# Two banks, a narrower gather and a later selection in the expert loop of a two-layer encoder trunk

## The chip, the cores and the metric

The kernel runs on one core of one Trainium2 chip. The metric is the device time of one execution in microseconds, the median of several; lower is better.

## What is computed

256 tokens of width 1024 go through two layers. Layer 0 is a latent attention and a dense SwiGLU, layer 1 a stick-breaking attention and a SwiGLU with 8 experts of which each token takes two. Everything is float32. The change touches the experts alone:

```
def swiglu(h, w_gate_up, w_down):
    g, u = jnp.split(h @ w_gate_up, 2, axis=-1)
    return (jax.nn.silu(g) * u) @ w_down
...
    for e in range(N_EXPERTS):
        y = y + gates[:, e:e + 1] * swiglu(xt, w_gate_up[e], w_down[e])
```

`w_gate_up[e]` is 1024 x 5632 and `w_down[e]` 2816 x 1024, so one expert has 34.6 MB of weights.

## The kernel before

The engines are programmed by hand, each with its own instruction list in a fixed order; semaphores join them. The expert layer is a list of items. An item is one expert and the tokens routed to it: a "big" item has 128 slots, a "small" one 64. Big and small items alternate, four pairs in this run (items 0 to 7); the last two pairs are in a loop with a run-time bound (`Fori`) and in the code behind it. A "pair" below is a big item and the small item after it.

**Units.** The weights of an item come as 33 units of 1 MB (22 of gate and up, 11 of down). SyncE's queue (SP) issues their transfers, in order, into a ring `raw` of 11 slots. It may fill a slot again when its content is used: in a big item when VectorE has made `wlo` of it (`lo_made`), in a small item when TensorE has finished with it (`small_used`). `after_big` and `big_loads` hold the first rule, `after_small` and `small_loads` the second. So the first 11 units of a small item (0 to 10) go into the slots that the last 11 units of the big item leave, and unit 11 waits until TensorE has finished unit 0 of the small item.

**Big item.** ScalarE rounds a unit to `whi` (L561), VectorE takes the rest as `wlo` (L962), both in a ring of 3 units; TensorE makes three products for each block of 512 columns (L1482 to L1484), 12 matmuls a unit. ScalarE may begin unit x+3 when TensorE has finished unit x (`used`). The 2816 hidden columns are made in groups j = 0 to 5 of 512 columns (the last of 256), with a gate half and an up half each; a half fills one bank of PSUM (512 columns), groups 0 and 1 are made in units 0 to 7, groups 2 and 3 in units 8 to 15, groups 4 and 5 in units 16 to 21. ScalarE takes silu of the gate half (L773, `silu_done`), VectorE multiplies by the up half (L1225, `gated`), TensorE transposes the product, and units 22 to 32 are the down product.

**Small item.** TensorE multiplies the raw float32 weights directly (L1487), 8 matmul instructions a unit in the trace, with no split before.

**Between items.** In down unit d = 5 of every item TensorE gathers the tokens of the next item: `gather` multiplies the token rows `xm` (stationary, 128 x 128) by a selection matrix `sel` (moving, 128 columns), 16 matmuls, of which a small item reads columns 0 to 63 only. ScalarE copies the result to `xs` for a small item or to `xhi` for a big one. `selection` then transposes `sel` into bank 6 (`TR_BANK`); it waits until all 8 copies are done, since they read banks 6 and 7, and stands behind down unit d = 8. After the last down unit `begin` computes units 0 and 1 of the next item, and then the item's result is spread back to the tokens ("scatter") in banks 4 to 7.

Of the kernel before, what the change touches and what calls it, by code (L numbers as in the profile page):

```python
# [14 lines left out]
P = 128  # L15
SEQ, D = 256, 1024
TC = SEQ // P
# [36 lines left out]
SMALL = 64  # L54
# [6 lines left out]
SUB = 6  # L61
# [5 lines left out]

def sub_bank(j):

    return (0, 2, 4, 0, 2, 7)[j]  # L70


SMALL_GROUPS = 4
# [62 lines left out]
def build(nc, t, out):  # L136
    with ExitStack() as ctx:
# [11 lines left out]
        xhi = sb("xhi", [P, KD, SEQ], F32R)  # L149
# [784 lines left out]
        def _(dve):  # L934
# [284 lines left out]
            def big(i, g, following):  # L1219

                def gate(j):
                    dve.wait_ge(silu_done[2], i * SUB + j + 1)
                    w = sub_width(j)
                    up = ps[:, sub_bank(j) + 1, :] if j < SUB - 1 else ps[:, sub_bank(j), w:2 * w]
                    V.tensor_tensor(gm[:, j % 2, 0:w], up, gm[:, j % 2, 0:w], ALU.mult).then_inc(gated[2], 1)  # L1225

                def low(j):
                    dve.wait_ge(h_hi[2], i * SUB + j + 1)
                    w = sub_width(j)
                    chunks = slice(4 * j, 4 * j + w // P)  # L1230
                    V.tensor_tensor(elo[:, chunks, :].rearrange("p a s -> p (a s)"), ps[:, TR_BANK, 0:w],
                                    ehi[:, chunks, :].bitcast(F32).rearrange("p a s -> p (a s)"), ALU.subtract).then_inc(h_lo[2], 1)

                for x in range(2, FU):
                    if x in (7, 15, 21):
                        gate({7: 0, 15: 2, 21: 4}[x])
                    if x in HIDDEN_AT:
                        low(HIDDEN_AT.index(x))
                    if x == 14:
                        item_gates(g)  # L1240
                        choose(g + 1, following)
                    if x == FU - 1:
                        for m in range(2):
                            dve.wait_ge(y_hi, i * 2 + m + 1)
                            V.tensor_tensor(xlo[:, 4 * m:4 * m + 4, P:SEQ], ps[:, 4 + m, :].rearrange("p (a s) -> p a s", a=4),
                                            xhi[:, 4 * m:4 * m + 4, P:SEQ].bitcast(F32), ALU.subtract).then_inc(y_lo, 1)
                    if x + 3 < FU or following == "big":
                        split_low_unit(H_MOE + RING + 2 * x, i)
                    if x in (7, 15, 21):
                        gate({7: 1, 15: 3, 21: 5}[x])  # L1250
                    if x == 29 and following == "big":
                        gathered_low(i + 1)
                if following == "big":
                    for x in range(3, 5):
                        split_low_unit(H_MOE + 2 * x, i + 1)
                add_in(g)
# [222 lines left out]
        def _(pe):  # L1479
# [248 lines left out]
                    if f == LAST_TR:  # L1728
                        transposes(n - 1)

            def gather(g):

                pe.wait_ge(sel_ready, g * 2 + 2)
                for k in range(KD):
                    o = ps[:, 6 + k // 4, (k % 4) * P:(k % 4 + 1) * P]
                    for c in range(TC):
                        last = mm(o, xm[:, c, k * P:(k + 1) * P], sel[:, c, :], c == 0 and k % 4 == 0, c == TC - 1)
                    if k % 4 == 3:
                        last.then_inc(gathered, 1)

            def big_unit(x, i, g):

                hh = H_MOE + 2 * x
                pe.wait_ge(lo_made, i * FH + hh + 2)
                whi_x, wlo_x = unit_split(whi, x), unit_split(wlo, x)
                if x < 16:
                    k = x % 8
                    if x < 8:
                        pe.wait_ge(xe_lo, i * KD + k + 1)
                    if x == 8:  # L1750
                        pe.wait_ge(h_ready[4], g * 4 + 4)
                    for n in range(2):
                        j = 2 * (x // 8) + n
                        if k == 0 and j == 3:
                            pe.wait_ge(gated[2], i * SUB + 1)
                        for a in range(2):
                            w = slice(a * 1024 + n * 512, a * 1024 + (n + 1) * 512)
                            last = mm3(ps[:, sub_bank(j) + a, :], xhi[:, k, 0:P], xlo[:, k, 0:P],
                                       whi_x[:, w], wlo_x[:, w], k == 0, k == KD - 1)
                        if k == KD - 1 and n == 0:  # L1760
                            last.then_inc(even_done, 1)
                else:
                    if x == 16:
                        pe.wait_ge(gated[2], i * SUB + 2)
                    for place, k, a in pieces(x, 4):
                        w = slice(place, place + 512)
                        last = mm3(ps[:, sub_bank(4) + a, :], xhi[:, k, 0:P], xlo[:, k, 0:P],
                                   whi_x[:, w], wlo_x[:, w], k == 0, k == KD - 1)
                    if x == GU - 1:
                        last.then_inc(even_done, 1)  # L1770
                    for place, k, a in pieces(x, 5):
                        w = slice(place, place + 256)
                        last = mm3(ps[:, sub_bank(5), a * 256:(a + 1) * 256], xhi[:, k, 0:P], xlo[:, k, 0:P],
                                   whi_x[:, w], wlo_x[:, w], k == 0 and a == 0, k == KD - 1)
                last.then_inc(used, 2)
# [43 lines left out]
            def big(i, g, following, next_i):  # L1819

                def transposes(j):
                    pe.wait_ge(gated[2], i * SUB + j + 1)
                    if j >= 1:
                        pe.wait_ge(h_lo[2], i * SUB + j)
                    w = sub_width(j)
                    for b, block in enumerate(interleaved(gm[:, j % 2, 0:w], j)):
                        last = pe.transpose(ps[:, TR_BANK, b * P:(b + 1) * P], block, ident[:, :])  # L1827
                    last.then_inc(gu_tr[2], 1)

                for x in range(2, GU):  # L1830
                    big_unit(x, i, g)
                    if x + 1 in HIDDEN_AT:
                        transposes(HIDDEN_AT.index(x + 1))
                for d in range(FU - GU):
                    hh = H_MOE + 2 * (GU + d)
                    pe.wait_ge(lo_made, i * FH + hh + 2)
                    if d % 2 == 0:
                        pe.wait_ge(h_lo[2], i * SUB + d // 2 + 1)
                    for m in range(2):
                        for n in range(2):  # L1840
                            f = 2 * d + n
                            w = slice(m * 512, (m + 1) * 512)
                            last = mm3(ps[:, 4 + m, :], ehi[:, f, :], elo[:, f, :],
                                       w_hi(hh + n)[:, w], w_lo(hh + n)[:, w], f == 0, f == FC - 1)
                    last.then_inc(used, 2)
                    if GU + d + 1 in HIDDEN_AT:
                        transposes(HIDDEN_AT.index(GU + d + 1))
                    if d == 5:
                        pe.wait_ge(h_lo[2], i * SUB + SUB)
                        gather(g + 1)  # L1850
                    if d == 8:
                        selection(following, next_i)
                begin(following, next_i, g + 1)
                pe.wait_ge(y_lo, i * 2 + 2)
                pe.wait_ge(selN_ready, g + 2)
                pe.wait_ge(selT_ready, g + 1)
                for c in range(TC):
                    for n in range(2):
                        o = ps[:, 4 + 2 * c + n, :].rearrange("p (a s) -> p a s", a=4)
                        w = selT[:, c * P:(c + 1) * P]  # L1860
                        mm(o, w, xhi[:, 4 * n:4 * n + 4, P:SEQ], True, False)
                        mm(o, w, xlo[:, 4 * n:4 * n + 4, P:SEQ], False, True).then_inc(scattered, 1)

            def small(p, g, following, next_i):
# [16 lines left out]
                for d in range(FU - GU):  # L1881
# [12 lines left out]
                        transposes(d + 1)  # L1894
                    if d == 5 and following is not None:
                        pe.wait_ge(hT_ready, p * SMALL_GROUPS + SMALL_GROUPS)
                        gather(g + 1)
                    if d == 8 and following is not None:
                        selection(following, next_i)
                if following is not None:  # L1900
# [100 lines left out]

            keep_clock(4, 4)
            pe.wait_ge(xm_ready, 2)
            gather(0)
            keep_clock(9, 4)
            begin("big", 0, 0)
            selection("big", 0)
# [32 lines left out]
```

## Time and profile before

| | us |
|---|---|
| median of 3 runs | 1138.62 (1137.79 to 1139.3) |
| the profiled execution's own time | 1135.15 |
| its span | 1133.4 |
| TensorE busy | 1083.6 |
| VectorE busy | 627.1 |
| ScalarE busy | 522.9 |
| bytes moved | 343.47 MB |

Times of single instructions are in microseconds from the start of the span. The expert items run from about 432 to 1123 us. A TensorE instruction's own length in the trace overlaps the next, so the time that one costs is read from the distance of two starts. "Idle before" is the time for which an engine stood still ahead of an instruction, with the work that ended it. The DMA share is the mean over 16 DMA engines and can be a little over 1.

### The profile page before, as it was taken

The numbers are of one execution on the slowest core, as the hardware profiler recorded it, in microseconds if no ns is written. First come the engines' busy times: TensorE is split into PE (matmuls) and PEld (weight loads), VectorE is DVE, ScalarE is ACT, GpSimd is POOL, SyncE is SP. The second block draws the span as 40 slices with busy tenths as digits, with TensorE's granted clock in tenths as the row PEclk, the third lists the DMA queues.
The fourth block names the chain that finished last, engine by engine and source line by source line (L and its number), as shares of the span: only waits on it lengthen the run. The fifth ranks groups of instructions, "written<-read, shape, count | busy, mean of one in ns | idle before, by whom it ended". The sixth has DMA issues, their size and how long they took to land.

```text
span 1133.4 us, 15880 instructions
## 1 busy us (share of the span) xinstructions
PE 1083.6 (96%) x5832; PEld 808.5 (71%) x5832; DVE 627.1 (55%) x712; ACT 522.9 (46%) x577; POOL 23.0 (2%) x94
## 2 busy tenths in 40 slices
PE   9998999999999999999998999998999999999994
PEld 9887888888898787787355787355787355787451
DVE  6866455555654458895116895106896106897102
ACT  6555444344445644774015774015775005776001
POOL 1100000000000000000000000000000000000000
PEclk9999999999999999999999999999999999999998
DMA  9933556555454424997999999999999999999994
GB/s 347 358 114 112 186 186 188 183 186 198 162 173 148 137 75 153 371 359 269 375 419 408 402 418 409 352 416 410 403 418 409 364 414 410 404 415 409 357 413 192
DMA packets 110935, 343.47 MB, mean 303 GB/s; under 512 B 11613, under 2 KB 38282, under 8 KB 100618
## 3 DMA queue, kind: packets, MB, share of 16 engines
q1 hardware_dynamic: 110714, 341.93, 79.9%
q8 instruction: 47, 0.77, 0.3%
q10 hardware_dynamic: 144, 0.52, 0.1%
q14 instruction: 30, 0.25, 0.1%
HBM read 341.37 MB, written 1.05 MB: 302 GB/s over the span
## 4 chain that ended last, share of the span: by engine, by line
PE 77%; DMA 7%; DVE 7%; ACT 3%; issue 2%; SPq 2%; POOL 0%; POOLq 0%; ACTq 0%; DVEq 0%
PE ps L1487 20%; PE ps L1482 18%; PE ps L1484 18%; PE ps L1483 18%; DMA raw<-moe_w_gate_up_dram 5%; DMA raw<-moe_w_down_dram 2%; SPq L368 2%; ACT whi L561 2%; DVE wlo L962 1%; PE ps L1827 1%; DVE wlo L949 1%; DVE wlo L951 1%; ACT xs L561 1%; DMA raw<-mla_w_down_dram 1%; DVE h L1144 1%
## 5 line engine op out<-in xcount | busy, mean ns | idle before, releaser
L561 ACT ACTIVATE whi<-raw 128x2048 fp32r<-128x2048 f32 (+2 forms) x203 | 341.7, 1688 | 245.8 <-PE ps L1484 226.8
L962 DVE TENSOR_TENSOR wlo<-raw,whi 128x2048 fp32r<-128x2048 f32 x151 | 345.7, 2294 | 119.5 <-ACT whi L561 118.3
L1482 PE MATMUL ps<-whi,xhi 128*128 128x512 f32 (+3 forms) x688 | 264.3, 384 | 16.3 <-DVE wlo L962 9.2
L1484 PE MATMUL ps<-wlo,xhi 128*128 128x512 f32 (+3 forms) x688 | 260.2, 378 | 0.0
L1483 PE MATMUL ps<-whi,xlo 128*128 128x512 f32 (+3 forms) x688 | 259.7, 377 | 0.0
L1482 PEld LDWEIGHTS ps<-whi,xhi 128*128 128x128 f32 x688 | 129.9, 189 | 45.2 <-DVE wlo L962 8.5
L1487 PE MATMUL ps<-raw,xs 128*64 128x512 f32 (+2 forms) x1024 | 155.0, 461 | 0.0
L1484 PEld LDWEIGHTS ps<-wlo,xhi 128*128 128x128 f32 x688 | 129.6, 188 | 23.9
L1483 PEld LDWEIGHTS ps<-whi,xlo 128*128 128x128 f32 x688 | 129.8, 189 | 22.5
L1487 PEld LDWEIGHTS ps<-raw,xs 128*64 128x64 f32 x1024 | 68.2, 137 | 81.7 <-issue 71.5
L1482 PE MATMUL ps<-whi,hhi 128*128 128x512 f32 x264 | 105.9, 401 | 0.0
L1483 PE MATMUL ps<-whi,hlo 128*128 128x512 f32 x264 | 104.3, 395 | 0.0
L1484 PE MATMUL ps<-wlo,hhi 128*128 128x512 f32 x264 | 104.3, 395 | 0.0
L949 DVE TENSOR_TENSOR wlo<-raw,whi 128x1024 fp32r<-128x1024 f32 (+1 forms) x52 | 60.2, 1170 | 52.2 <-ACT whi L561 52.2
L1487 PE MATMUL ps<-raw,hT 128*64 128x512 f32 x352 | 80.6, 598 | 4.1 <-DMA raw<-moe_w_down_dram 4.0
L1264 DVE TENSOR_TENSOR gu<-ps,gu 128x512 f32<-128x512 f32 (+2 forms) x16 | 8.0, 522 | 133.3 <-ACT gu L810 133.3
L810 ACT ACTIVATE gu<-ps 128x512 f32<-128x512 f32 (+2 forms) x16 | 7.0, 463 | 125.5 <-PE ps L1487 125.5
L951 DVE SCALAR_TENSOR_TENSOR wlo<-raw,gcol,whi 128x1024 fp32r<-128x1024 f32 (+1 forms) x34 | 41.5, 1236 | 32.1 <-ACT whi L561 32.0
L1484 PEld LDWEIGHTS ps<-wlo,hhi 128*128 128x128 f32 x264 | 49.5, 187 | 12.0
L561 ACT ACTIVATE whi<-raw,gcol 128x1024 fp32r<-128x1024 f32 (+1 forms) x34 | 37.5, 1112 | 43.5 <-PE ps L1484 43.5
L1482 PEld LDWEIGHTS ps<-whi,hhi 128*128 128x128 f32 x264 | 49.6, 188 | 11.0
L1483 PEld LDWEIGHTS ps<-whi,hlo 128*128 128x128 f32 x264 | 49.6, 188 | 11.0
(299 smaller groups left out, 972.3 us busy)
## 6 DMA issues: line engine op xcount, KB each, us to landing
raw<-moe_w_gate_up_dram SPq DMA_DIRECT2D x256, 512.0 KB, 12.7
raw<-moe_w_down_dram SPq DMA_DIRECT2D x80, 1024.0 KB, 17.1
raw<-moe_w_gate_up_dram SPq DMA_DIRECT2D x96, 384.0 KB, 9.4
raw<-ffn_w_gate_up_dram SPq DMA_DIRECT2D x44, 512.0 KB, 4.9
raw<-ffn_w_down_dram SPq DMA_DIRECT2D x22, 512.0 KB, 4.3
raw<-kv_shared_w_dram SPq DMA_DIRECT2D x16, 512.0 KB, 4.2
raw<-moe_w_gate_up_dram SPq DMA_DIRECT2D x32, 256.0 KB, 9.6
raw<-moe_w_down_dram SPq DMA_DIRECT2D x16, 512.0 KB, 17.7
```

The costliest lines, as they stand in the source:

```text
L368: sp_eng.dma_start(raw[:, u % RAW, place:place + n], w_gu[k * P:(k + 1) * P, a * FF + c:a * FF + c + n]).then_inc(landed[u % RAW], 16)
L561: return nc.scalar.activation(o, i, ACT.Copy, scale=scale)
L949: V.tensor_tensor(w_lo(hh)[:, 0:w], raw_half(hh), hi, ALU.subtract).then_inc(lo_made, 1)
L951: V.scalar_tensor_tensor(out=w_lo(hh)[:, 0:w], in0=raw_half(hh), scalar=gcol[:, g:g + 1], in1=hi, op0=ALU.mult, op1=ALU.subtract).then_inc ...
L962: V.tensor_tensor(wlo[:, s, :].rearrange("p a w -> p (a w)"), raw[:, (hh // 2) % RAW, :], whi[:, s, :].bitcast(F32).rearrange("p a w -> p ...
L1144: V.tensor_tensor(hv, ps[:, bank(c, n), :], hv, ALU.add).then_inc(ready, 1)
L1264: V.tensor_tensor(gm[:, j % 2, 0:w], up, gm[:, j % 2, 0:w], ALU.mult).then_inc(small_gated, 1)
L1482: pe.matmul(o, a_hi, b_hi, start=start, stop=False, skip_group_check=True)
L1483: pe.matmul(o, a_lo, b_hi, start=False, stop=False, skip_group_check=True)
L1484: return pe.matmul(o, a_hi, b_lo, start=False, stop=stop, skip_group_check=True)
L1487: return pe.matmul(o, a, b, start=start, stop=stop, skip_group_check=True)
L1827: last = pe.transpose(ps[:, TR_BANK, b * P:(b + 1) * P], block, ident[:, :])
```

## The change

It does three things in the expert items, and nothing outside them.

First, the banks of a big item's groups. Group 3 had its gate half in bank 0 and its up half in bank 1, the banks of group 0; now its gate half is in bank 7, its up half in bank 0. Group 5 (both halves in one bank) moves from bank 7 to bank 1. In unit 8 TensorE therefore no longer waits for VectorE's product of group 0 (`gated`) ahead of group 3's gate half, but for ScalarE's silu of group 0 (`silu_done`) ahead of its up half.

Second, the gather for a small item uses 64 moving columns in place of 128.

Third, in a big item the selection stands behind down unit d = 9, not d = 8.

```
 def sub_bank(j):
-    return (0, 2, 4, 0, 2, 7)[j]
+    return (0, 2, 4, 7, 2, 1)[j]
+
+def up_bank(j):
+    return (1, 3, 5, 0, 3, 1)[j]
...
-            def gather(g):
+            def gather(g, slots):
...
-                    o = ps[:, 6 + k // 4, (k % 4) * P:(k % 4 + 1) * P]
+                    o = ps[:, 6 + k // 4, (k % 4) * P:(k % 4) * P + slots]
                     for c in range(TC):
-                        last = mm(o, xm[:, c, k * P:(k + 1) * P], sel[:, c, :], c == 0 and k % 4 == 0, c == TC - 1)
+                        last = mm(o, xm[:, c, k * P:(k + 1) * P], sel[:, c, 0:slots], c == 0 and k % 4 == 0, c == TC - 1)
...
                         j = 2 * (x // 8) + n
-                        if k == 0 and j == 3:
-                            pe.wait_ge(gated[2], i * SUB + 1)
                         for a in range(2):
+                            if k == 0 and j == 3 and a == 1:
+                                pe.wait_ge(silu_done[2], i * SUB + 1)
                             w = slice(a * 1024 + n * 512, a * 1024 + (n + 1) * 512)
-                            last = mm3(ps[:, sub_bank(j) + a, :], xhi[:, k, 0:P], xlo[:, k, 0:P],
+                            last = mm3(ps[:, up_bank(j) if a else sub_bank(j), :], xhi[:, k, 0:P], xlo[:, k, 0:P],
                                        whi_x[:, w], wlo_x[:, w], k == 0, k == KD - 1)
...
                     if d == 5:
                         pe.wait_ge(h_lo[2], i * SUB + SUB)
-                        gather(g + 1)
-                    if d == 8:
+                        gather(g + 1, SMALL if following == "small" else P)
+                    if d == 9:
                         selection(following, next_i)
```

TensorE in unit 8 of the first big item, before: the two halves of group 3, gate first, three matmuls each.

```order
L1484 MATMUL ps<-wlo,xhi 128x512
L1482 MATMUL ps<-whi,xhi 128x512 [waits gated2]
L1483 MATMUL ps<-whi,xlo 128x512
L1484 MATMUL ps<-wlo,xhi 128x512
L1482 MATMUL ps<-whi,xhi 128x512
L1483 MATMUL ps<-whi,xlo 128x512
```

The same place after the change:

```order
L1488 MATMUL ps<-wlo,xhi 128x512
L1486 MATMUL ps<-whi,xhi 128x512
L1487 MATMUL ps<-whi,xlo 128x512
L1488 MATMUL ps<-wlo,xhi 128x512
L1486 MATMUL ps<-whi,xhi 128x512 [waits silu_done2]
L1487 MATMUL ps<-whi,xlo 128x512
```

The wait is three matmuls later, and for another engine.

TensorE at the gather behind down unit d = 5 of the first big item, before and then after:

```order
L1484 MATMUL ps<-wlo,hhi 128x512
L1487 MATMUL ps<-sel,xm 128x128 [waits sel_ready,h_lo2]
L1487 MATMUL ps<-sel,xm 128x128 x15
L1482 MATMUL ps<-whi,hhi 128x512 [waits h_lo2,lo_made]
L1483 MATMUL ps<-whi,hlo 128x512
```

```order
L1488 MATMUL ps<-wlo,hhi 128x512
L1491 MATMUL ps<-sel,xm 128x64 [waits sel_ready,h_lo2]
L1491 MATMUL ps<-sel,xm 128x64 x15
L1486 MATMUL ps<-whi,hhi 128x512 [waits h_lo2,lo_made]
L1487 MATMUL ps<-whi,hlo 128x512
```

The 16 gather matmuls stay where they are and write 64 columns each.

TensorE at the selection of the first big item, before (between down units d = 8 and d = 9) and then after (between d = 9 and d = 10):

```order
L1483 MATMUL ps<-whi,hlo 128x512
L1484 MATMUL ps<-wlo,hhi 128x512
L1808 MATMUL ps<-ident,sel 128x128 [waits xs_ready]
L1808 MATMUL ps<-ident,sel 128x128
L1482 MATMUL ps<-whi,hhi 128x512 [waits lo_made]
L1483 MATMUL ps<-whi,hlo 128x512
```

```order
L1487 MATMUL ps<-whi,hlo 128x512
L1488 MATMUL ps<-wlo,hhi 128x512
L1812 MATMUL ps<-ident,sel 128x128 [waits xs_ready]
L1812 MATMUL ps<-ident,sel 128x128
L1486 MATMUL ps<-whi,hhi 128x512 [waits h_lo2,lo_made]
L1487 MATMUL ps<-whi,hlo 128x512
```

The two transposes have moved back by one unit of 12 matmuls. The lists of ScalarE, VectorE, GpSimd and SyncE keep their order and their waits; only the bank that some of their instructions read is another.

## Rows read from the trace of the kernel before

**Rows 1.** The page: span, TensorE's busy time, GB/s in 40 slices.
```profile
span 1133.4 us, 15880 instructions
...
PE 1083.6 (96%) x5832; PEld 808.5 (71%) x5832; DVE 627.1 (55%) x712; ACT 522.9 (46%) x577; POOL 23.0 (2%) x94
...
GB/s 347 358 114 112 186 186 188 183 186 198 162 173 148 137 75 153 371 359 269 375 419 408 402 418 409 352 416 410 403 418 409 364 414 410 404 415 409 357 413 192
```

**Rows 2.** The chain that ended last: start, us, what.
```profile
761.40 17.33 DMA raw<-moe_w_gate_up_dram
778.80 1.94 ACT whi L561
...
1095.63 22.28 DMA raw<-moe_w_down_dram
```

**Rows 3.** Windows, POOL only: us, POOL busy, PEclk, DMA share, GB/s.
```profile
534.00:539.00 5.00, 0.00 (x0) 1.00 0.24 54
616.00:707.00 91.00, 0.00 (x0) 1.00 1.03 410
708.00:713.00 5.00, 0.00 (x0) 1.00 0.62 193
...
711.00:712.00 1.00, 0.00 (x0) 1.00 0.79 86
...
881.00:885.00 4.00, 0.00 (x0) 1.00 0.73 238
...
1053.00:1058.00 5.00, 0.00 (x0) 1.00 0.70 229
```

**Rows 4.** SP's issues and its wait there; the small item's first matmuls.
```profile
703.14 0.85 SPq L368 DMA_DIRECT2D raw<-moe_w_gate_up_dram  x2
...
708.23 3.65 PE L1487 MATMUL ps<-raw,xs 128*64 128x512 f32 x16
...
710.35 0.85 SPq L368 DMA_DIRECT2D raw<-moe_w_gate_up_dram  x2
...
SPq L368 <- PE ps L1487: 6.2, 1, 6.2
```

**Rows 5.** TensorE in unit 8, pair 2; its waits over all items (total, times, longest).
```profile
631.06 0.39 PE L1484 MATMUL ps<-wlo,xhi 128*128 128x512 f32 x1
632.45 0.50 PE L1482 MATMUL ps<-whi,xhi 128*128 128x512 f32 x1 [1.01 <-DVE gu L1225]
...
PE ps L1482 <- DVE gu L1225: 4.0, 4, 1.0
...
PE ps L1808 <- ACT xs L561: 3.7, 4, 0.9
```

**Rows 6.** ScalarE and VectorE at that place: silu of group 0; wlo of unit 10.
```profile
629.31 0.57 ACT L773 ACTIVATE gu<-ps 128x512 f32<-128x512 f32 x1
...
632.32 2.28 DVE L962 TENSOR_TENSOR wlo<-raw,whi 128x2048 fp32r<-128x2048 f32 x1
```

**Rows 7.** TensorE: gather of 128 columns, and router products of 8 columns.
```profile
689.20 3.73 PE L1487 MATMUL ps<-sel,xm 128*128 128x128 f32 x32
692.69 0.48 PE L1482 MATMUL ps<-whi,hhi 128*128 128x512 f32 x1
...
419.33 1.85 PE L1487 MATMUL ps<-router,xr 128*128 128x8 f32 x16
421.03 0.80 PE L1487 MATMUL ps<-ident 128*128 128x128 f32 x5
```

**Rows 8.** TensorE and ScalarE around the selection of pair 2.
```profile
700.94 0.39 PE L1484 MATMUL ps<-wlo,hhi 128*128 128x512 f32 x1
702.26 0.44 PE L1808 MATMUL ps<-ident,sel 128*128 128x128 f32 x2 [0.93 <-ACT xs L561]
702.45 0.48 PE L1482 MATMUL ps<-whi,hhi 128*128 128x512 f32 x1
...
700.48 1.73 ACT L561 ACTIVATE xs<-ps,gcol 128x64 f32<-128x64 f32 x8
```

More of the change, by code:

```diff
@@ L1223, in gate @@
                     w = sub_width(j)
-                    up = ps[:, sub_bank(j) + 1, :] if j < SUB - 1 else ps[:, sub_bank(j), w:2 * w]
+                    up = ps[:, up_bank(j), :] if j < SUB - 1 else ps[:, up_bank(j), w:2 * w]
                     V.tensor_tensor(gm[:, j % 2, 0:w], up, gm[:, j % 2, 0:w], ALU.mult).then_inc(gated[2], 1)
@@ L1766, in big_unit @@
                         w = slice(place, place + 512)
-                        last = mm3(ps[:, sub_bank(4) + a, :], xhi[:, k, 0:P], xlo[:, k, 0:P],
+                        last = mm3(ps[:, up_bank(4) if a else sub_bank(4), :], xhi[:, k, 0:P], xlo[:, k, 0:P],
                                    whi_x[:, w], wlo_x[:, w], k == 0, k == KD - 1)
@@ L1896, in small @@
                         pe.wait_ge(hT_ready, p * SMALL_GROUPS + SMALL_GROUPS)
-                        gather(g + 1)
+                        gather(g + 1, P)
                     if d == 8 and following is not None:
@@ L2003, in _ @@
             pe.wait_ge(xm_ready, 2)
-            gather(0)
+            gather(0, P)
             keep_clock(9, 4)
```

## The prediction

> **What bounds the kernel now.** I read the page first. TensorE is busy for 96% of the span [rows 1], and one could stop there: a TensorE-bound kernel, and every microsecond taken from TensorE is a microsecond of the end. But the GB/s line says something else. From the 21st slice on it stands at 400 to 420, with a dip to about 355 in every sixth or seventh. The eight experts weigh 8 x 34.6 = 277 MB, and at 410 GB/s that is 675 us, about all of the time that the items take. So I went to the chain that ended last. At the turn from a small item to a big one it runs through a transfer of 17.3 us into ScalarE's `whi`, and in the last item it is one transfer of 22.3 us that TensorE waits for at the end [rows 2]. A unit of 1 MB (1.05e6 bytes) takes 2.56 us at 410 GB/s, so a transfer of 17 us is not slow, it stands in a queue of some six units. The start of each big item, and the end of the kernel, are set by the transfers.
>
> The windows give the rest. Between 616 and 707 us the DMA engines are full (share 1.03, 410 GB/s) [rows 3], though ScalarE, VectorE and TensorE work there on a ring whose slots are all taken. Only one place in each pair is not full: the first microseconds of the small item. There the five microseconds from 708 carry 193 GB/s, in the other pairs 54 (from 534), 238 (four from 881) and 229 (five from 1053) [rows 3]. The reader is to see why in SP's rows: the issue at 703.14 fills the last slot that the big item has left (unit 10). The next one, unit 11, is issued at 710.35, after a wait of 6.2 us for TensorE's L1487 [rows 4]. That is the end of the small item's unit 0: eight matmuls from 708.23, half of the 3.65 us of the sixteen, so 710.05, and 0.3 us more for the semaphore. Meanwhile the queue has run dry; the engines come back at about 711.2 (share 0.79 in 711 to 712) [rows 3], 0.9 us after the issue.
>
> So a pair lasts as long as its 66 units of transfers at full rate, plus one hole. Let me count a hole in lost microseconds at 410 GB/s: pair 1: 5 x (1 - 54/410) = 4.3; pair 2: 5 x (1 - 193/410) = 2.65; pair 3: 4 x (1 - 238/410) = 1.7; pair 4: 5 x (1 - 229/410) = 2.2 [rows 3]. The hole ends when TensorE has done the small item's unit 0, and TensorE's way to there starts with the landing of the big item's first units. What shortens TensorE's work inside the big item therefore comes off the hole, microsecond for microsecond, until the hole is closed; beyond that it is worth nothing.
>
> **The change, part by part.**
>
> The banks. Now TensorE stops in unit 8 for VectorE's product of group 0: idle 1.01 us, four times, 4.0 us in all [rows 5]. Starts go from 631.06 to 632.45, 1.39 us, where matmuls of 512 columns follow each other every 0.23 us (3.65 for sixteen, [rows 4]): it costs 1.16 us. After the change the wait is for silu of group 0 alone, which runs from 629.31 for 0.57 us [rows 6] and so ends at 629.9, ahead even of the gate half. The wait goes to nothing. What is late next? TensorE comes 1.16 us sooner to unit 10, whose `wlo` is made from 632.32 to 634.60 [rows 6]. Unit 9 starts six matmuls after 632.45, at 633.9, and so at 632.7 in the new order; with 12 x 0.23 = 2.75 us of its own, and some tenths for the transposes behind it, unit 10 is wanted at 635.5 or later. That leaves 0.9 us. Later units follow TensorE's own pace (`used`), so their distances stay. Value: 1.16 us a pair; bounds 0 (all of it waited again at another unit) and 1.3 (a restart takes a little longer than 0.23 us as well).
>
> The selection. TensorE's last matmul before it starts at 700.94, the first behind it at 702.45 [rows 8]: 1.51 us where 0.23 would be without it, so 1.28 us, of which 0.93 is the wait for ScalarE's eight `xs` copies (3.7 us over four) [rows 5, 8]. These are done at 700.48 + 1.73 = 702.2. One unit later TensorE comes there at about 701.2 + 2.8 = 704.0, 1.8 us after they are done, so the wait is gone and the two transposes remain: 0.2 us by 702.26 to 702.45, 0.35 with what the row before them loses (1.28 - 0.93). Value: 0.95 us; bounds 0.9 and 1.1.
>
> The gather. Now 32 instructions (each of the 16 matmuls stands twice in the trace) from 689.20 to 692.69: 3.49 us, 109 ns each [rows 7]. Does half the columns mean half the time? No row has 64 columns with a full stationary operand, but there is one with 8: the router's products, 16 instructions from 419.33 to 421.03, 106 ns each [rows 7]. Both load a stationary operand of 128 x 128. With 8 columns the price is that of 128, so columns aren't what it goes by, and 64 lie between 106 and 109: a gain of 0 to 0.1 us. I take 0.1. The other end, were it by columns after all, is half of 3.49, a gain of 1.75 us; I keep it as a rival.
>
> The Trainium skill weighs in on both sides of this. "TensorE: Matmul & The Clock Gate", section "Back-to-back issue gap", has an isolated gap of N/2.4 + 2.5 ns, 56 ns for 128 columns and about half for 64; by it the gather would get cheaper by nearly half. The section "LDWEIGHTS" of the same page has a load of P/1.2, an estimate of 107 ns for 128 stationary columns whatever moves. The trace's 109 and 106 ns agree with the second.
>
> The moved wait has nothing new behind it on TensorE but its own units, and ScalarE, VectorE, GpSimd and SyncE have the same lists. The gather for a big item is as before.
>
> **The sum.** TensorE's way to the small item's unit 0 gets 1.16 + 0.95 + 0.1 = 2.2 us shorter in each pair. Against the holes: pair 1 gives 2.2 (its hole is 4.3), pair 2 2.2 (of 2.65), pair 3 1.7 (all of its hole), pair 4 2.2 (of 2.2): 8.3 us. The last transfers of a queue don't end all at once, so a little of each closed hole will remain; I take off 0.1 each: 7.9 us. That is 0.7% of the profiled execution's own time of 1135.15 us (its span of 1133.4 and 1.75 around it), which would come to 1127.3. The median of the three runs shown is 1138.62, 3.5 us above that execution, and I carry that difference along: 1138.6 - 7.9 = 1130.7.
>
> Bounds. If a closed hole keeps a microsecond of slow start each (0.8 us of full rate is missing in 711 to 712 alone, at 86 GB/s), the gain is 8.3 - 4 = 4.3 at worst, 1134.3. If no tail is left and the banks bring 1.3, the holes give 2.4 + 2.4 + 1.7 + 2.2 = 8.7 and the slow start after them may give 0.3 each more: 9.9, or 1128.7.
>
> **The rivals.**
>
> A. The bank part is given back: TensorE, 1.2 us ahead, waits at one of units 9 to 15 for `wlo`. For it: ScalarE has silu of groups 0 and 1 between its splits there, and the 0.9 us that I counted are thin. Against it: `wlo` of unit 10 is early by the rows. Then 1.05 us a pair are left, all inside the holes: 4.2 us, 1134.4.
>
> B. The transfers are the bound and a closed hole opens elsewhere in the pair, since the ring of 11 slots only passes it on. For it: the rate is 410 GB/s in full windows, and these are most of the pair. Against it: outside the holes nothing is missing from 616 to 707, so units that come sooner find free slots. Only pair 1, which begins with a full ring, would gain 2.2: 1136.4, just within 0.2% of 1138.6 (2.3 us, about what a measurement of this kernel can tell from no change).
>
> C. The gather goes by columns: 1.65 us more from TensorE in each pair. Pair 1's hole takes it all (4.3 against 3.9), pair 2 has 0.45 left, the others nothing: 7.9 + 1.65 + 0.45 = 10.0, 1128.6. The router's row speaks against it.
>
> D. Slower: the selection's second use. The transposed selection is copied by ScalarE and needed by the scatter, behind `begin`. In the present clock it moves from 702.3 to 705.1, one unit; the scatter starts at 708.23 + 3.65 = 711.9 [rows 4, 8], so 6.8 us remain for a copy that is smaller than a silu of 0.57 us [rows 6]. Were the copy held up for longer, TensorE would wait at the scatter. That lies behind unit 1, so it would spare the hole, but it delays the units after it, and with them every slot. To come out slower by over 2.3 us it must take back 7.9 and add 2.3, 2.6 us in each of four pairs: a copy that is 9.4 us late. ScalarE has nothing but the last copies there. The point is far off; as an example, a delay of 10 us would give 1141.5.
>
> **How the numbers follow.** My forecast (7.9, from 6.5 to 9.3) gets 0.62; A 0.14; B 0.10; C 0.09; D and whatever else slows it 0.05. The predicted time is 1130.7. The range is to hold it 8 times in 10: from C's 1128.3 to a little above A, 1134.6, which leaves out B, D and the outer part of the forecast. The forecast alone would go from 1129.3 to 1132.1. Faster by over 0.2%: forecast, A, C and a small part of B, 0.88; within 0.2%: most of B and a little of D, 0.08; slower: 0.04.
>
> **What would show it.** In the profile after, TensorE's rows have no wait for L1229 (the product, now four lines down) in unit 8, and none for `xs` at the selection. The gather's 32 instructions still take 3.4 us or more. SP's issue of the small item's unit 11 comes 2.2 us sooner, counted from the landing of the big item's first unit, and the windows of 5 us at the big to small turns of pairs 2 to 4 carry over 350 GB/s, that of pair 1 about 230. A pair, from unit 11's issue to the next one's, takes about 170 us (66 units at 2.56 us are 168.8). TensorE is busy for the same time in a shorter span, and it waits more often for transfers late in the small items, since it is there sooner than they are. I am wrong if the holes close and the pairs keep their length (B), if a new wait of 0.5 us or more for `wlo` stands in units 9 to 15 (A), or if the gather takes 1.8 us (C).

## The result, and the profile after

| | before | after |
|---|---|---|
| median, us | 1138.34 (5 runs, 1136.46 to 1139.3) | 1126.88 (5 runs, 1125.91 to 1129.17) |
| ratio | | 0.9901 (0.9888 to 0.9915) |
| profiled execution's own time | 1135.15 | 1129.17 |
| its span | 1133.4 | 1127.3 |

The change makes the kernel 11.5 us faster, 1.0%. I had forecast 7.9 us, and the range ended at 1128.3. The way was right, the size was too small.

The page after:

```profile
span 1127.3 us, 15880 instructions
...
PE 1084.9 (96%) x5832; PEld 812.4 (72%) x5832; DVE 626.4 (56%) x712; ACT 522.6 (46%) x577; POOL 23.5 (2%) x94
...
GB/s 347 361 115 113 187 187 187 187 187 187 153 184 149 123 102 83 381 363 320 329 415 409 404 416 409 389 414 410 404 415 410 399 413 411 404 414 409 393 413 191
```

TensorE is busy for the same time as in [rows 1]; the dips of the GB/s line, about 355 before, are 389 to 399.

TensorE's waits over the expert part (total, times, longest):

```profile
PE ps L1486 <- DVE wlo L966: 7.9, 5, 2.1
PE ps L1491 <- DMA raw<-moe_w_down_dram: 4.1, 6, 1.3
PE ps L1491 <- issue: 2.5, 3, 0.8
PE ps L1491 <- DVE ys L1279: 0.8, 1, 0.8
```

Against [rows 5] the two lines for the product and for `xs` are gone, 7.7 us, and nothing of their size has come in. (Line numbers are four higher than before.)

TensorE in unit 8, pair 2, across the place where it stood still for 1.01 us:

```profile
631.97 0.39 PE L1488 MATMUL ps<-wlo,xhi 128*128 128x512 f32 x1
632.20 0.39 PE L1486 MATMUL ps<-whi,xhi 128*128 128x512 f32 x1
632.43 0.39 PE L1487 MATMUL ps<-whi,xlo 128*128 128x512 f32 x1
```

The starts are 0.23 us apart. Before, the stop cost 1.39 - 0.23 = 1.16 us by the first two starts, and 0.11 more, since the first matmul behind a stop is followed after 0.34 us and not 0.23. So it was 1.27.

The gather for the small item, and the selection (now between d = 9 and d = 10), pair 2:

```profile
688.81 3.68 PE L1491 MATMUL ps<-sel,xm 128*128 128x64 f32 x32
692.30 0.48 PE L1486 MATMUL ps<-whi,hhi 128*128 128x512 f32 x1
...
703.36 0.40 PE L1488 MATMUL ps<-wlo,hhi 128*128 128x512 f32 x1
703.59 0.38 PE L1812 MATMUL ps<-ident,sel 128*128 128x128 f32 x2
703.73 0.48 PE L1486 MATMUL ps<-whi,hhi 128*128 128x512 f32 x1
```

The gather takes 3.49 us, exactly as in [rows 7]: nothing gained by half the columns. The selection costs 703.73 - 703.36 - 0.23 = 0.14 us instead of 1.28: 1.14 us gained.

SP's queue at the turn of pair 2, and its wait there:

```profile
702.75 0.85 SPq L372 DMA_DIRECT2D raw<-moe_w_gate_up_dram  x2
...
708.82 0.85 SPq L372 DMA_DIRECT2D raw<-moe_w_gate_up_dram  x2
...
SPq L372 <- PE ps L1491: 5.8, 2, 5.1
```

The windows there, and at the turns of pairs 1, 3 and 4 (columns as in [rows 3]):

```profile
535.00:540.00 5.00, 0.00 (x0) 1.00 0.45 120
...
704.00:709.00 5.00, 0.00 (x0) 1.00 1.02 409
...
709.00:714.00 5.00, 0.61 (x1) 1.00 0.96 363
...
879.00:884.00 5.00, 0.61 (x1) 1.00 1.03 394
...
1050.00:1055.00 5.00, 0.61 (x1) 1.00 0.99 369
```

Where 193, 238 and 229 GB/s stood in [rows 3] there are now 363, 394 and 369. The holes of pairs 2 to 4 are nearly closed in these windows; that of pair 1 is still open. The prediction wanted about 230 GB/s there; 534 to 539, its own window, carries 171 after the change.

The holes are longer than those windows. Over 25 us from just before each small item, in the kernel before and then after:

```profile
705.00:730.00 25.00, 0.61 (x1) 1.00 0.94 348
877.00:902.00 25.00, 0.61 (x1) 1.00 0.97 360
1049.00:1074.00 25.00, 0.61 (x1) 1.00 0.95 351
```

```profile
703.00:728.00 25.00, 0.61 (x1) 1.00 1.01 389
873.00:898.00 25.00, 0.61 (x1) 1.00 1.02 400
1044.00:1069.00 25.00, 0.61 (x1) 1.00 1.02 393
```

Counted as the prediction counts (25 x (1 - 348/410) and so on), pairs 2 to 4 missed 3.8, 3.0 and 3.6 us of transfers before and miss 1.3, 0.6 and 1.0 after: 2.4 to 2.6 us of each hole have been closed.

How long each stretch takes is best read from the first matmuls of the small items. They stand in both timelines as a group of sixteen; the start of the first big item and the last item's scatter bound them. After:

```profile
435.40 0.47 PE L1486 MATMUL ps<-whi,xhi 128*128 128x512 f32 x1 [0.37 <-DVE xlo L1191]
...
535.76 3.65 PE L1491 MATMUL ps<-raw,xs 128*64 128x512 f32 x16
...
706.70 3.65 PE L1491 MATMUL ps<-raw,xs 128*64 128x512 f32 x16
...
876.51 3.65 PE L1491 MATMUL ps<-raw,xs 128*64 128x512 f32 x16
...
1047.08 3.65 PE L1491 MATMUL ps<-raw,xs 128*64 128x512 f32 x16
...
1114.61 1.56 PE L1491 MATMUL ps<-ys,selT 64*128 64x512 f32 x6 [0.80 <-DVE ys L1279]
```

And before (the second small item's is in [rows 4]):

```profile
432.41 0.47 PE L1482 MATMUL ps<-whi,xhi 128*128 128x512 f32 x1 [0.38 <-DVE xlo L1187]
...
535.13 3.65 PE L1487 MATMUL ps<-raw,xs 128*64 128x512 f32 x16
...
880.11 3.65 PE L1487 MATMUL ps<-raw,xs 128*64 128x512 f32 x16
...
1052.98 3.65 PE L1487 MATMUL ps<-raw,xs 128*64 128x512 f32 x16
...
1120.69 1.56 PE L1487 MATMUL ps<-ys,selT 64*128 64x512 f32 x6 [0.79 <-DVE ys L1275]
```

In the table, "small 1" is the first small item, and the differences are those of these starts, with those of the experiments below from the same rows of their timelines:

| us | first big item | small 1 to 2 | 2 to 3 | 3 to 4 | small 4 to end | expert part |
|---|---|---|---|---|---|---|
| before | 102.72 | 173.10 | 171.88 | 172.87 | 67.71 | 688.28 |
| after | 100.36 | 170.94 | 169.81 | 170.57 | 67.53 | 679.21 |
| after, second profile | 100.35 | 170.59 | 169.77 | 170.26 | 67.47 | 678.44 |
| gather of 64 columns only | 102.71 | 173.54 | 172.78 | 172.90 | 67.86 | 689.79 |
| banks only | 101.51 | 171.69 | 171.21 | 171.98 | 67.80 | 684.19 |
| selection only | 101.60 | 171.51 | 171.33 | 171.67 | 67.74 | 683.85 |
| banks and selection | 100.30 | 170.87 | 169.47 | 170.58 | 67.59 | 678.81 |
| after, 12 of 16 gather products left out | 97.64 | 166.88 | 169.97 | 171.05 | 70.25 | 675.79 |
| after, lighter transfers | 100.33 | 169.24 | 168.59 | 168.58 | 65.62 | 672.36 |
| after, both | 97.65 | 166.00 | 165.93 | 165.91 | 65.66 | 661.15 |
| before, big items' transfers lighter | 102.74 | 172.71 | 173.07 | 172.73 | 67.85 | 689.10 |
| before, small items' transfers lighter | 102.71 | 171.55 | 170.98 | 171.28 | 65.04 | 681.56 |
| before, unit 0 early | 99.93 | 172.42 | 172.44 | 172.72 | 71.42 | 688.93 |
| after, unit 0 early | 97.51 | 169.47 | 169.88 | 170.63 | 70.35 | 677.84 |

In the last two rows the small item's first unit stands 2.8 us earlier in the program, so their first column is shorter and the last longer by that for this reason alone.

Between the two profiles the expert part is 9.1 us shorter: 2.36 in the first big item, 2.16, 2.07 and 2.30 in the three pairs, 0.18 at the end.

### The profile page after: what moved, and what is told of

The parts are those of the page before. It is cut to its first block, busy times and chain, and to the rows that moved or that the text cites. A ratio compares the mean times of both kernels' runs of the same rounds, so it can differ in the third digit from the quotient of the medians.

```text
span 1127.3 us, 15880 instructions
## 1 busy us (share of the span) xinstructions
PE 1084.9 (96%) x5832; PEld 812.4 (72%) x5832; DVE 626.4 (56%) x712; ACT 522.6 (46%) x577; POOL 23.5 (2%) x94
## 2 busy tenths in 40 slices
DMA packets 110935, 343.47 MB, mean 305 GB/s; under 512 B 11613, under 2 KB 38282, under 8 KB 100618
## 3 DMA queue, kind: packets, MB, share of 16 engines
HBM read 341.37 MB, written 1.05 MB: 304 GB/s over the span
## 4 chain that ended last, share of the span: by engine, by line
PE 80%; DMA 7%; DVE 7%; SPq 2%; ACT 1%; issue 1%; POOL 0%; POOLq 0%; ACTq 0%; DVEq 0%
PE ps L1491 20%; PE ps L1486 19%; PE ps L1488 19%; PE ps L1487 19%; DMA raw<-moe_w_gate_up_dram 5%; DMA raw<-moe_w_down_dram 2%; SPq L372 2%; DVE wlo L966 1%; PE ps L1831 1%; DVE wlo L953 1%; DVE wlo L955 1%; ACT whi L565 1%; DVE h L1220 1%; DVE h L1148 1%; DMA raw<-mla_w_down_dram 1%
## 5 line engine op out<-in xcount | busy, mean ns | idle before, releaser
L1491 PEld LDWEIGHTS ps<-raw,hT 128*64 128x64 f32 x352 | 23.3, 136 | 47.8 <-issue 34.8
```

The costliest lines, as they stand in the source:

```text
L1491: return pe.matmul(o, a, b, start=start, stop=stop, skip_group_check=True)
```

## The experiments

All ratios are to the kernel before, timed on the same chip in the same rounds.

**The three parts alone.** The first kernel has the bank tables, the split `up_bank` and the moved wait, as in the diff above, and nothing else.

> Only the bank part. Theory (TensorE's way inside the big item is shortened and the pair gets shorter by that until the hole in the transfers closes): TensorE saves 1.27 us a pair in unit 8, the expert part gets 4.9 us shorter (4.5 to 5.2). Rival 1 (the gain of 11.5 in the medians has a further part that is not in the waits): 6 us or more. Rival 2 (wait given back): under 2 us.

Measured: 1132.46 us, before 1137.39; ratio 0.9953 (0.9938 to 0.9967). That is 4.9 us in the median. The theory put 4.9 on the expert part, which is 4.1 us shorter than in the profile of before (684.19 against 688.28), 1.21 of it in the first big item.

The second has the selection alone:

```
-                    if d == 8:
+                    if d == 9:
                         selection(following, next_i)
```

> Only the later selection. Theory: TensorE saves 1.1 us a pair, 4.3 us in all (4.0 to 4.7). Rival 1 (more in it than the waits): 6 us or more. Rival 2 (a later wait takes its place): under 2 us.

Measured: 1132.34, ratio 0.9954 (0.994 to 0.9969): 5.05 us, a little over the 4.7; the expert part is 4.4 us shorter, 1.12 of it in the first big item.

The third has the gather alone:

```
-                        last = mm(o, xm[:, c, k * P:(k + 1) * P], sel[:, c, :], c == 0 and k % 4 == 0, c == TC - 1)
+                        last = mm(o, xm[:, c, k * P:(k + 1) * P], sel[:, c, 0:slots], c == 0 and k % 4 == 0, c == TC - 1)
```

> Only the gather with 64 columns. Theory (the price is that of loading the stationary 128 x 128): 32 instructions in 3.49 us as with 128 columns, time as before within 0.1%. Rival (by columns): 1.75 us less TensorE time a pair, 6 to 7 us less in all.

Measured: 1137.71, ratio 1.0003 (0.9992 to 1.0014). Its timeline at the gather of pair 2:

```profile
690.88 3.68 PE L1487 MATMUL ps<-sel,xm 128*128 128x64 f32 x32
694.37 0.48 PE L1482 MATMUL ps<-whi,hhi 128*128 128x512 f32 x1
```

3.49 us again, 109 ns for each instruction, with 64 columns as with 128. The rival C of the prediction is out.

The fourth has banks and selection.

> Banks and selection, the gather as before. Theory: the whole of the change, an expert part that is 9.1 us shorter, and the same median as the changed kernel within 0.7 us. Rival (the gather brings the 2.4 us by which the median gained more than the two profiles): 2 us or more above the changed kernel.

Measured: 1127.69, ratio 0.9905 (0.9887 to 0.9923). The two parts together give 9.7 us, the two alone 4.9 + 5.05, and the changed kernel's ratio lies in this interval: the gather adds nothing that can be told.

**The changed kernel again.**

> The changed kernel once more, unaltered, to tell the median's gain of 11.5 us from the 9.1 us by which its profiled expert part is shorter. Theory (the first medians had chance in them, since the part ahead of the experts varies by 4 us from run to run): 9 to 10.5 us under the kernel before. Rival (there is a further gain that profiles don't show): 11 us or more.

Measured: 1125.35, before 1137.61; ratio 0.9898 (0.988 to 0.9916), a gain of 12.3 us by the medians and 11.6 by the ratio. That is over the theory's 9 to 10.5, of which the upper part lies in the interval (9.5 to 13.7 us), and speaks rather for the rival. Its profile has an expert part of 678.44 us. The kernels that have none of the change's savings (before, gather only, lighter big items) have 688.28, 689.79 and 689.10, so the profile of before that I read was the shortest of its kind; against the mean of the three, 689.06, and of the two of after, 678.83, the change is worth 10.2 us there. The intervals of both measurements (9.7 to 12.7 us and 9.5 to 13.7) hold 10.2 too. The remaining microsecond or so between profiles and medians isn't explained; a further gain that profiles don't show isn't ruled out.

**Two bounds.** A kernel whose transfers run at full rate nearly all the time and whose TensorE is 96% busy may be bound by either. The next three begin from the changed kernel. The first takes work off TensorE by leaving out 12 of the 16 products in the gather for a small item:

```
-                for k in range(KD):
+                for k in range(KD) if slots == P else (3, 7):
```

> The changed kernel, and in the gather for a small item only 4 of the 16 products are computed (12 are left out), which takes 2.6 us more off TensorE in each pair. Theory (the change has closed the holes in the transfers of pairs 2 to 4, and a pair of 66 units can't be shorter than 168.8 us): pair 1 brings 2.6, the others 0.2 to 0.9 each, 4 us in all (3 to 5.5) beside the changed kernel. Rival (TensorE alone sets the pace): 2.6 us in each of four pairs, 10.5 us.

Measured: 1123.7, ratio 0.9876 (0.9856 to 0.9895); beside the changed kernel's 1126.88 it is 3.2 us less, not 10.5. In the table the first big item is 2.7 us shorter and the stretch from small item 1 to 2 four, more than the 2.6 taken off there, for which no run has the reason; but the next two are no shorter and the end is 2.7 us longer. What the transfers don't allow is waited for instead, by the first of TensorE's waits (total, times, longest):

```profile
PE ps L1491 <- DMA raw<-moe_w_down_dram: 9.2, 15, 1.4
```

9.2 us in 15 waits, where the changed kernel has 4.1 in 6.

The second takes transfers away: of two of each item's eleven down units only the first half is loaded.

```
-                    sp_eng.dma_start(raw[:, u % RAW, :], of).then_inc(landed[u % RAW], 16)
+                    n = HALF if light and x in (29, 30) else 2 * HALF
+                    sp_eng.dma_start(raw[:, u % RAW, 0:n], of[:, 0:n]).then_inc(landed[u % RAW], 16)
```

> The changed kernel, and of down units 29 and 30 of every item only the first half is transferred (0.5 MB each; the products there use stale numbers), 2.56 us of transfers less in each item. Theory (transfers and TensorE are within 1 us of each other at every turn): 0.5 to 0.8 us at each of three turns and 2.5 us at the end, where TensorE waits for the last units: 4 to 5 us beside the changed kernel. Rival 1 (transfers alone set the pace): 5.1 us a pair, about 18 us. Rival 2 (TensorE alone): the end's 2.5 us only.

Measured: 1120.92, ratio 0.9847 (0.9826 to 0.9869): 6.0 us less than the changed kernel. More than 4 to 5, far less than 18. The turns give 1.2 to 2.0 us each, not 0.5 to 0.8.

The third does both.

> The changed kernel with both: 4 of 16 gather products for a small item, and half of units 29 and 30 in every item. Theory (each of the two bounds hides the other's gain): more than the sum of the two alone, TensorE's 2.6 us now count in every pair: 10.5 + 4.5 = 15 us (13 to 17) beside the changed kernel. Rival (one bound only): no more than the two alone together.

Measured: 1110.24, ratio 0.9753 (0.9731 to 0.9775): 16.6 us less than the changed kernel, where the two alone give 3.2 + 6.0 = 9.2. Each bound hid part of what was saved on the other, 7.4 us of it. With lighter transfers the pairs are at 168.6 us with the change and at 165.9 with 2.7 us less of TensorE work, so 168.6 is TensorE's own way through a pair. Adding the 2.4 us that the change took off TensorE, I estimate 171.0 us for the kernel before.

**Which transfers count in the kernel before.** Same edit as above, but only for big items and in the kernel before:

> The kernel before, and of units 29 and 30 of the big items behind the first only the first half is transferred (2.56 us of transfers less in each of these three items). Theory (as long as there is a hole, it is TensorE that ends it, so transfers saved before the hole only widen it): under 1 us. Rival (a pair lasts as long as its transfers and the hole): 2.56 us in each of three pairs, 7 us less.

Measured: 1137.53 against 1137.19, ratio 1.0003 (0.9989 to 1.0016). The lighter transfers are in all four big items and not in three: the run moves 339.28 MB, 4.19 less than 343.47, and that is four times 1.05. 2.56 us fewer transfers in each big item change nothing. They only widen the hole behind them, by 2.1 to 2.6 us:

```profile
705.00:730.00 25.00, 0.61 (x1) 1.00 0.87 312
878.00:903.00 25.00, 0.61 (x1) 1.00 0.87 318
1051.00:1076.00 25.00, 0.61 (x1) 1.00 0.87 316
```

The rival named in the expectation isn't quite the prediction's account. There too it is TensorE that ends the hole, so that fewer bytes ahead of it bring nothing.

And only for small items:

> The kernel before, and of units 29 and 30 of the small items only the first half is transferred (the products there use stale numbers). The counterpart of the run with lighter big items, which changed nothing. Theory (in the kernel before, transfers hold TensorE up only where it turns from a small item to a big one, and there 1.6 us a pair lie over TensorE's own way): 1.6 us at each of three turns and 2 to 2.5 us at the end, 6.5 us less than before (5 to 8). Rival (before the change TensorE alone sets the pace of the pairs): the end's 2 to 2.5 us only.

Measured: 1129.12 against 1138.02, ratio 0.992 (0.9906 to 0.9933): 8.9 us less, a little over the 5 to 8, and far over the rival's 2.5. The pairs are at 171.55, 170.98 and 171.28 us. At the turn to a big item ScalarE's fourth `whi` had waited for a transfer before; here it waits for TensorE. Before, and then with lighter small items:

```profile
782.48 1.92 ACT L561 ACTIVATE whi<-raw 128x2048 fp32r<-128x2048 f32 x1 [1.76 <-DMA raw<-moe_w_gate_up_dram]
```

```profile
781.84 1.92 ACT L562 ACTIVATE whi<-raw 128x2048 fp32r<-128x2048 f32 x1 [1.72 <-PE ps L1485]
```

So transfers held up the kernel before as well, but those of the small items, at the turn to the big one, and by 1 to 2 us a pair.

**Is the hole a cause?** TensorE computes unit 0 of the small item ahead of the last down unit, which is meant to issue unit 11 sooner by 2.8 us; nothing is taken off TensorE (the edit also lets the later loop begin at unit 3):

```
-                begin(following, next_i, g + 1)
+                    if d == 9:
+                        small_unit(0, next_i, g + 1)
+                for x in (1, 2):
+                    small_unit(x, next_i, g + 1)
```

In the kernel before:

> The same early unit in the kernel before, with its waits in unit 8 and at the selection in place. The holes close by 2.8 us each with no work taken off TensorE. Theory (TensorE's own way from one small item to the next sets the pair, the hole is only what is left over): 2 to 3 us less than before, nearly all at the end. The prediction's account (a pair is its transfers and the hole, so a closed hole shortens the pair): 2.8 + 2.65 + 1.7 + 2.2 = 9 us less.

Measured: 1135.83 against 1137.61, ratio 0.998 (0.997 to 0.9991): 1.8 us less (2.3 by the ratio), not 9. Its profile doesn't show even that: the expert part is 688.93 us, where kernels without the change have 688.28 to 689.79. The windows of its trace at the turn of pair 2:

```profile
705.00:710.00 5.00, 0.00 (x0) 1.00 1.02 406
710.00:715.00 5.00, 0.00 (x0) 1.00 0.83 301
```

The place of the old hole is full, and the missing bytes have moved to 710 and after. SP's rows show why. Unit 11 is issued at 707.89, 2.5 us sooner than before. But the unit behind it waits for TensorE's unit 1, which still stands behind all down units, and it is issued at 712.75, where it was 712.06 before:

```profile
707.89 0.85 SPq L368 DMA_DIRECT2D raw<-moe_w_gate_up_dram  x2
...
712.75 0.85 SPq L368 DMA_DIRECT2D raw<-moe_w_gate_up_dram  x2
```

Over the 25 us of each turn nearly as much is missing as before, 3.3, 3.4 and 3.5 us in place of 3.8, 3.0 and 3.6:

```profile
705.00:730.00 25.00, 0.61 (x1) 1.00 0.97 356
878.00:903.00 25.00, 0.61 (x1) 1.00 0.96 355
1050.00:1075.00 25.00, 0.61 (x1) 1.00 0.95 353
```

So this run moves the hole and doesn't close it. That the pairs keep their length says nothing against the prediction's account; the 9 us of the expectation were never on offer.

In the changed kernel:

> The changed kernel, and TensorE computes unit 0 of the small item ahead of the big item's last down unit, and unit 2 with unit 1 behind it; the amount of work is the same, but unit 11's transfer is issued 2.8 us sooner. Theory (of both bounds the transfers are short by 0.1 to 0.3 us a pair and by up to 2.5 us at the end): 2 to 3.5 us less than the changed kernel. Rival (TensorE alone sets the pace): within 0.5 us of it.

Measured: 1125.1, ratio 0.9892 (0.9874 to 0.9909), against 1125.35 for the changed kernel in the same rounds. The 2 to 3.5 us that I expected are not there; the rival's number (within 0.5 us) is what came, though the run with fewer transfers rules out the rival's reason, TensorE alone. I had counted on 2.5 us at the end; I suppose that the last item's waits for transfers come from a queue that is full already, in which an earlier issue only stands longer, but no run shows it. Why the kernel with the short gather gains 2.7 us in its expert part (675.79 against 678.44) and this one 0.6 (677.84) I can't say; both issue unit 11 of the first small item 2.5 to 2.8 us sooner.

## Why the prediction was wrong in size

**What bounds the kernel: the path was right, with one thing missing.** The prediction lets a pair run through the small item's transfers to the big item's first units, and from there over TensorE to the small item's unit 0. The runs bear it out in the main: fewer bytes in the big items brought nothing, fewer bytes in the small items 8.9 us, and TensorE's 2.4 us came off the pairs. What it lacks is how close TensorE's own way lies in the small item as well. Of 2.56 us saved in a small item's transfers 1.6 arrived at each turn, against the mean of the three profiles of the kind before; the pairs ended at 171.0 to 171.6 us, and TensorE's own way is an estimated 171.0. And "only one place in each pair is not full" doesn't hold for pair 1: between 495 and 520 us, inside the first big item, the kernel before moves 344 GB/s, and between 525 and 530 us 122.

**The banks: right in mechanism, 0.11 us too small.** I took 1.16 us and named 1.3 as the upper end; it is 1.27, with the slow restart. Alone it shortens the first big item by 1.21 us and the kernel by 4.9. Rival A, a new wait in units 9 to 15, didn't come.

**The selection: right, 0.19 us too small.** I took 0.95 us; it is 1.14, since the two transposes cost 0.14 and not 0.35 us when TensorE isn't stopped at them. Alone it gives 5.05 us.

**The gather: right.** I took 0.1 us from 106 against 109 ns; it is 0.00.

**The sum: the cap by the holes failed.** TensorE's saving is 1.27 + 1.14 = 2.4 us a pair, not 2.2; the profiles show 2.36 in the first big item. That is 0.8 us over four pairs. And I cut the saving by the size of the hole and by 0.1 for its tail, 0.9 us in all. The holes were taken from windows of four and five microseconds, 2.65, 1.7 and 2.2 us; over 25 us they are 3.8, 3.0 and 3.6. The slow stretch behind each window (367 and 351 GB/s in 885 to 895 before) belongs to the hole. So 2.4 us fit into every hole, that of pair 3 too, which I had let give 1.6; by the starts it gave 2.07 or, with the second profile, 2.11, and against the mean of three profiles of its kind 2.8. Without the cut the sum is 4 x 2.4 = 9.6; the profiles have 9.1, or 10.2 by the means.

**From the profile to the median: the other step that failed.** With 9.6 the forecast would have been 1129.0, still inside the range. I carried the 3.5 us between median and profiled execution along unchanged: the median of before lies 3.2 us above its profiled execution, that of after 2.3 us below. Together that is 5.5 us. Three of them are the start of the first big item, at 432.41 us in the one profile and 435.40 in the other, with the same code ahead of it. Another 1.2 are the expert part, by which the two profiles differ by 9.1 us and the means by 10.2; the pair from small item 2 to 3 took 171.88 us in the profile of before, where two others of its kind show 172.78 and 173.07. Up to 1.3 us stay open, and the cause of what carried the time below the range is known only in part.

**Rivals.** A (a new wait) and D (slower) are out, and B (the change only moves the hole) by the windows over 25 us. C is out by two measurements, the unchanged time of the gather and the run with the gather alone. Two slips: the range begins at "C's 1128.3", where C's own sum is 1128.6; and D's example of a delay of 10 us comes to 1143.5 by its own terms (4 x 3.2 - 7.9 = 4.9 us slower), not 1141.5.

## What to carry to other kernels

When a queue of transfers is full but for one hole in each round, the hole's size tells what the round is longer than its bytes, and not who makes it so. Measure it up to where the rate is back, here over 25 us and not 5, before you cap a saving by it. And a transfer that is issued sooner may only move the hole, if the next one still waits. The test is a pair of runs, one with fewer bytes and one with less work, and one with both: if both together gain more than the sum, two bounds lie close together, and a further saving on one side alone will be mostly lost (of the 10.5 us taken off TensorE in the changed kernel, 3.2 arrived). A narrower moving operand saves nothing on TensorE where each instruction loads a full stationary float32 operand.

## What the runs showed of the hardware

The products of a 128 x 128 float32 stationary operand follow each other every 106 to 109 ns with 8, 64 and 128 moving columns (3.49 us for 32 with 64 and with 128, [rows 7]), and about every 214 ns with 512 columns and a stationary operand of 64 columns. That is (3.65 - 1.94)/8, from sixteen and eight of them in one trace; 3.65 us is the time from the first start to the last end, so a sixteenth of it is too much. The prediction's 0.23 us is right for the products of the big items, by their starts. From the kernel before with unit 0 early:

```profile
705.77 1.94 PE L1487 MATMUL ps<-raw,xs 128*64 128x512 f32 x8
...
710.63 3.65 PE L1487 MATMUL ps<-raw,xs 128*64 128x512 f32 x16
```

I had expected little from 64 columns, but not exactly nothing. The Trainium skill, "TensorE: Matmul & The Clock Gate", section "LDWEIGHTS", gives a load of P/1.2 ns, by which 128 columns are an estimate of 107. The three spacings agree with it; the trace's own records of these loads are longer, 192 ns each in the gather, and overlap.

The stage ahead of the first big item (router and first gather) runs at half of TensorE's clock for a part of the time in some executions of the same code. The granted clock is the third number from the right here; first the changed kernel, then the kernel before:

```profile
422.00:428.00 6.00, 6.00 (x36) 0.61 0.00 0
```

```profile
422.00:428.00 6.00, 6.00 (x52) 1.00 0.00 0
```

0.61 is a mean of the two levels, 2.4 and 1.2 GHz. TensorE is busy all of these six microseconds in both and works off 36 instructions in the one and 52 in the other. The first big item starts at 435.40 and at 432.41 us; over the fourteen profiles of this study it starts between 431.7 and 435.9. The start follows the clock: the four profiles with 1.00 in this window start by 432.4, the five with 0.76 to 0.86 at 433.2 to 433.7, the five with 0.58 to 0.61 at 435.0 or later. For a comparison of a few microseconds between two profiles, that is as much as the thing to be measured, and it has nothing to do with the change.
